# A transformer block in split float32 on one core: another order of work at the end of each MLP block, and of the loads behind the first MLP product

## The reference

```python
sh_a, sc_a, gt_a, sh_m, sc_m, gt_m = [m[:, None, :] for m in jnp.split(mod, N_MOD, axis=-1)]
...
h = rms_norm(x, g_pre_mlp[l]) * (1.0 + sc_m) + sh_m
y = jnp.square(jax.nn.relu(h @ w_mlp_in[l])) @ w_mlp_out[l]
x = x + gt_m * rms_norm(y, g_post_mlp[l])
```

## Time and profile before

| | us |
|---|---|
| median of 3 runs (2080.5 to 2085.15) | 2080.77 |
| the profiled execution | 2085.15 |
| its span, first to last instruction | 2083.5 |
| TensorE busy | 2025.0 (97%) |
| VectorE busy | 1717.7 (82%) |
| ScalarE busy | 992.3 (48%) |

### The profile page before, as it was taken

How to read it: one execution, slowest core, us unless ns; L and a number is a source line. 1 busy time by engine, 2 the same in 40 slices (tenths; PEclk the granted TensorE clock), 3 DMA queues, 4 the chain that set the end, 5 groups by cost and what they waited for, 6 DMA issues and landing times.

```text
span 2083.5 us, 30862 instructions
## 1 busy us (share of the span) xinstructions
PE 2025.0 (97%) x11186; PEld 1762.6 (85%) x11186; DVE 1717.7 (82%) x2013; ACT 992.3 (48%) x1403; POOL 156.4 (8%) x163
## 2 busy tenths in 40 slices
PE   7999999999999989999999999999999999999998
PEld 6887888877888868889999999998778888888886
DVE  5986898788876768689999999987788888888866
ACT  5554322578833365455555656654333333333322
POOL 0000000057600000000000000000020000000000
PEclk9999999999999999999999999999999999999999
DMA  9996869610286744757667666677656456446452
GB/s 308 341 310 221 272 204 256 200 31 1 72 293 213 264 149 139 241 179 235 216 218 231 214 231 214 216 241 287 256 211 242 179 184 242 181 181 249 174 182 81
DMA packets 294238, 435.37 MB, mean 209 GB/s; under 512 B 30181, under 2 KB 176265, under 8 KB 285321
## 3 DMA queue, kind: packets, MB, share of 16 engines
q1 hardware_dynamic: 276008, 361.43, 52.3%
q0 software_dynamic: 16704, 67.11, 8.8%
q10 hardware_dynamic: 1440, 5.70, 0.7%
HBM read 367.09 MB, written 67.11 MB: 208 GB/s over the span
## 4 chain that ended last, share of the span: by engine, by line
PE 77%; DVE 9%; DMA 5%; issue 4%; ACT 4%; SPq 1%; DVEq 0%; ACTq 0%
PE bank L2841 8%; PE bank L2843 8%; PE bank L2842 8%; PE bank L2863 7%; PE bank L2865 7%; PE bank L2864 7%; PE bank L2382 4%; PE bank L2384 4%; PE bank L2383 4%; PE bank L2395 2%; PE bank L2396 2%; PE bank L2397 2%; DMA raw<-in_w_ada 2%; DMA raw<-in_w_out 1%; PE bank L2921 1%
## 5 line engine op out<-in xcount | busy, mean ns | idle before, releaser
L2863 PE MATMUL bank<-hi,y_use 128*128 128x512 f32 x784 | 310.2, 396 | 13.6 <-DVE lo L2198 8.0
L1366 ACT ACTIVATE hi<-w 128x1024 fp32r<-128x1024 f32 x168 | 178.3, 1062 | 295.9 <-PE bank L2865 217.7
L2864 PE MATMUL bank<-lo,y_use 128*128 128x512 f32 x784 | 306.7, 391 | 0.0
L2865 PE MATMUL bank<-hi,y_use 128*128 128x512 f32 x784 | 306.6, 391 | 0.0
L1280 ACT ACTIVATE hi<-a 128x1024 fp32r<-128x1024 f32 x182 | 191.8, 1054 | 147.3 <-DVE a L2079 126.1
L2076 DVE TENSOR_TENSOR lo<-a,hi 128x1024 fp32r<-128x1024 f32 x182 | 221.9, 1219 | 43.9 <-ACT hi L1280 43.6
L837 ACT ACTIVATE hi<-raw 128x1024 fp32r<-128x1024 f32 (+2 forms) x132 | 129.1, 993 | 269.9 <-DMA raw<-in_w_in 93.7
L2198 DVE TENSOR_TENSOR lo<-w,hi 128x1024 fp32r<-128x1024 f32 x168 | 205.3, 1226 | 39.8 <-ACT hi L1366 38.2
L2841 PE MATMUL bank<-h_hi,hi 128*128 128x256 f32 x832 | 235.6, 283 | 0.0
L2842 PE MATMUL bank<-h_lo,hi 128*128 128x256 f32 x832 | 235.5, 283 | 0.0
L2843 PE MATMUL bank<-h_hi,lo 128*128 128x256 f32 x832 | 235.4, 283 | 0.0
(11 more groups left out here) (378 smaller groups left out, 4719.1 us busy)
## 6 DMA issues: line engine op xcount, KB each, us to landing
raw<-in_w_ada SPq DMA_DIRECT2D x166, 512.0 KB, 5.3
w<-in_w_mlp_out SPq DMA_DIRECT2D x128, 512.0 KB, 4.8
y_dram<-y_out POOLq DMA_DIRECT2D x32, 1792.0 KB, 6.8
y_use<-y_dram SPq DMA_DIRECT2D x53, 1024.0 KB, 8.8
a<-in_w_mlp_in SPq DMA_DIRECT2D x104, 512.0 KB, 4.5
raw<-in_w_in SPq DMA_DIRECT2D x32, 512.0 KB, 5.7
raw<-in_w_out SPq DMA_DIRECT2D x32, 512.0 KB, 5.0
gate_row<-in_w_ada SPq DMA_DIRECT2D x26, 512.0 KB, 5.1
```

The costliest lines, as they stand in the source:

```text
L2863: mm(bank[b + m][:], yh, hi[s][:, q, :], start=j == 0, stop=False)
L2864: mm(bank[b + m][:], yh, lo[s][:, q, :], start=False, stop=False)
L2865: ins = mm(bank[b + m][:], yl, hi[s][:, q, :], start=False, stop=j == PAIRS - 1)
```

## The change

It reorders four lists and neither adds nor removes an instruction. SyncE, at the boundary: the two halves of w21 and the last gate row are issued ahead of the first two y loads, the first half of w21 ahead of more weights. ScalarE, in each su block but the first: pair_hi goes ahead of snap 2 and su_hi 6. VectorE, at the end of each su block: su_low 0 of the next block ahead of its sum_one, and its sum_three behind corner 2 and su_low 2. VectorE, first half of the down phase: third(0) ahead of unit_lo(0), as in all other halves.

```diff
@@ -707,20 +707,20 @@
             end = SLOTS * (SU_BLOCKS - 1)
             sp.wait_ge(su_mixed, 4 * SU_BLOCKS - 1)
             weights(0, 0, "22", (0,))
+            sp.wait_ge(su_mixed, 4 * SU_BLOCKS)
+            weights(0, 0, "21", (0,))
             sp.wait_ge(su_lo, end + 5)
             weights(0, 0, "22", (1,))
             sp.wait_ge(w_used, SU_W + end + 2)
             weights(0, 0, "11")
             weights(0, 0, "12")
+            sp.wait_ge(su_lo, end + 6)
+            weights(0, 0, "21", (1,))
+            gate_behind(LAST, PAIRS - 1)
             sp.wait_ge(w_used, SU_W + end + 3)
             sp.wait_ge(y_saved, 16 * PAIRS)
             values(0, 0)
             values(0, 1)
-            sp.wait_ge(su_mixed, 4 * SU_BLOCKS)
-            weights(0, 0, "21", (0,))
-            sp.wait_ge(su_lo, end + 6)
-            weights(0, 0, "21", (1,))
-            gate_behind(LAST, PAIRS - 1)
             sp.wait_ge(w_used, DN_W)
             for k in (2, 3, 4):
                 values(0, k)
@@ -1324,10 +1324,10 @@
                 su_hi(g, i, 5)
                 if first:
                     square_pair(SU_FIRST - 1)
+                else:
+                    pair_hi(g, i - 1)
                 snap(g, i, 2)
                 su_hi(g, i, 6)
-                if not first:
-                    pair_hi(g, i - 1)
                 if final:
                     unit_hi(0, 0, 0)
                     unit_hi(0, 0, 1)
@@ -2139,14 +2139,14 @@
                 if final:
                     corner(g, i, 1)
                     return
+                su_low(g, i + 1, 0)
                 sum_one(g, i + 1)
-                su_low(g, i + 1, 0)
                 corner(g, i, 1)
                 su_low(g, i + 1, 1)
                 sum_two(g, i + 1)
-                sum_three(g, i + 1)
                 corner(g, i, 2)
                 su_low(g, i + 1, 2)
+                sum_three(g, i + 1)
                 if first:
                     pair_lo(g, i - 1)
 
@@ -2225,12 +2225,8 @@
                     wait_dn(dve, w_mixed, g, np, 8, 5 + h)
                     mix(dw["21"][np][h], dw["21"][np][h], dw["11"][np][h], ALU.subtract)
 
-                if first:
-                    unit_lo(0)
-                    third(0)
-                else:
-                    third(0)
-                    unit_lo(0)
+                third(0)
+                unit_lo(0)
                 third(1)
                 unit_lo(1)
                 one(0)
```

## The result

The kernel after takes 2101.85 us (median of 4 runs, 2100.46 to 2103.17), the kernel before, run beside it, 2080.64 (4 runs, 2080.5 to 2085.15). The ratio is 1.0098 (95% interval 1.0083 to 1.0113): 21.2 us slower. The forecast was 2089.6, with a range up to 2099. The direction held; the time lies outside the range.

A forecast was written before the change was run, and what follows sets the result against it. TensorE, busy 97%, was taken as the bound, time changing only through its waits. Loop + 16.4, second block + 0.4 and boundary - 8.0 gave + 8.8 us: 2089.6 against the median of 2080.77, range 2078 to 2099.

The forecast's parts named there:

- What bounds the kernel: Whole kernel: TensorE is busy 97% of the span, so time is lost or won only where it waits.
- The loop, + 16.4: su blocks: the path through VectorE and ScalarE closes at 20.95 us, 21 blocks wait, together 16.4 us slower.
- the walk: su block: measured start-to-start steps summed once around the longest path through VectorE and ScalarE, giving 20.95 us against 20.16.
- The second block, + 0.4: Where ScalarE's squares wait for pair_lo: between 1.2 us better and 0.8 worse, walked as 0.4 worse.
- SyncE at the boundary, - 8.0: After the su blocks: gate row lands earlier, 4.99 us gap goes, next gap shrinks, clock may stay up; 8.0 us gained.
- the delay of the values: Boundary: values 0, queued behind w21 half 1 and the gate row, land 2.6 or 3.3 us later, taken as 3.0.
- the earlier store: Boundary: pair_lo of the last pair, its store and the ten weight loads behind it move 4.6 us earlier.
- the boundary gives nothing back: Rival, boundary: values 0 land 5 us later, TensorE stops there, clock drops twice as before; 2097.6 us, chance 0.10.
- the four: Whole kernel: own forecast 2089.6 (0.72); rivals no closed path 2073.2 (0.12), boundary 2097.6 (0.10), lowered clock 2109 (0.06).
- third(0), nothing: First half of the down phase: unit_lo(0) moves to about 1427, covered because TensorE needs it only with values 0; no cost.
- The rival of a lowered clock in each block: su blocks: each short wait lowers the clock, 21 blocks lose 1.7 us each, + 36, total 2109 us; chance 0.06.

The follow-up runs named there:

- The two runs that split VectorE's edit: Kernel before with pair_hi moved up, plus either only sum_three behind su_low 2 (2084.21 us) or only su_low 0 ahead of sum_one (2115.72 us).
- the run with su_low 0 first: Kernel before with pair_hi moved up and su_low 0 ahead of sum_one, sum_three left in place: 2115.72 us, a single profiled execution.
- one number changed here: Kernel before with gate_part of the last block hung behind unit 7 in place of unit 2, no load moved: 2078.1 us, ratio 0.9977.

## Why the prediction was wrong in size

**What bounds the kernel: right.** What was lost or won beyond the scatter was TensorE's waiting, at the places named.

**The loop, + 16.4: right, 16.9.** Blocks of 20.91 to 20.99 (20.95 forecast), TensorE waiting for corner 1 (c_b), su_low 6 waiting 0.73 for ScalarE (0.75 forecast), pair_hi waiting for y_mix. The third block lost 1.03 where 0.65 was forecast; the second, which was to just meet its need, already waited 1.06 for corner 1. The path with ScalarE's edit alone came out as 20.55 to 20.63 (20.6), with VectorE's alone as 20.16 (closed). The two runs that split VectorE's edit moved the block in opposite directions, each to the length that the walk gave beforehand (20.16 and 21.48); neither a fixed cost for each edit nor VectorE's busy time, 18.45 to 18.61 us in a block of each of these kernels, does that. VectorE's 8% of idle time was no room for this order.

**The second block, + 0.4: wrong, + 2.3.** "ScalarE's squares wait there for pair_lo" was the only wait named. pair_hi, moved up, also waits for its output buffer: 3.47 us for the store of y, with snap 2 and su_hi 6 now behind it. ScalarE's edit alone has 1.8 of it, VectorE's alone 0.5. The bound given, 0.8 worse, was too narrow.

**SyncE at the boundary, - 8.0: this is the step that failed; it gave 2.2 at most, by the ratio of SyncE's edit alone 0.6.** Two terms of it were wrong, the delay of the values and the earlier store. On the first the sentence was "They land later by 1.05 MB at 410 GB/s, 2.6 us, or 3.3 us", and the loads landed 6.4 to 6.9 us later. The bytes were right and half 0 was rightly left out (0.54 us of waiting with it alone). The rate was wrong. In the run of SyncE's edit alone, from 1424.9 to 1434.4 (TensorE stood for the last 6.6 us of it), with the store of y under way, the queues carried (packets, MB, share of the DMA engines):

```profile
q1 hardware_dynamic: 420, 2.47, 62.1%
q0 software_dynamic: 387, 1.57, 40.1%
```

q1 moved 2.47 MB in 9.5 us, 260 GB/s, and not all of it for the loads up to the one waited for. The 1.05 MB cost about 6 us, 175 GB/s: w21 half 1 and the gate row landed 5.6 us behind the load ahead of them. The 410 of the earlier trace rows is both queues together, and the 317 of the earlier trace rows is a mean over 26 us of which the store takes only a part. Before the store's first packets q1 had the engines to itself, here in the kernel before, 1418.2 to 1424.2 us, 370 GB/s:

```profile
q1 hardware_dynamic: 947, 2.22, 102.8%
```

The store's first packets come 17.1 to 17.8 us behind the last block's start in all fourteen profiles, and the first y load landed at +20.4 before. So what was put ahead of it was paid for in the store's stretch. The Trainium skill (DMA: Bandwidth & Descriptors, Queues, rings and completion order) gave the direction, that descriptors of a ring are consumed in order, and the runs agree; the estimate of 2.9 us from its HBM limit did not hold (6.4 to 6.9 measured), since that limit is for all queues and one of them was asked for; all together they reached 410 to 428 GB/s in windows of this case. What the prediction left unused stands in the same section of that page: each DMA engine takes turns between the queues that have work, a packet at a time. The two rows agree (420 packets on q1, 387 of the store, which had 39% of the bytes), and read that way a load on q1 never has the whole rate while the store runs.

The second term was "pair_lo of the last pair, its store, SyncE's wait for that store ... and the ten weight loads behind it move 4.6 us earlier". Counted from the last block's start the store was issued at +41.0 where it was +41.1, and ScalarE shows why: the weight units ahead of pair_lo now wait for TensorE, which started 6.9 us late. The store before and after, and the first of these waits:

```profile
1449.36 0.94 POOL L3049 DMA_DIRECT2D y_dram<-y_out  x1 [27.28 <-DVE y_out L2033]
1466.88 0.94 POOL L3045 DMA_DIRECT2D y_dram<-y_out  x1 [27.15 <-DVE y_out L2033]
1457.62 1.06 ACT L1366 ACTIVATE hi<-w 128x1024 fp32r<-128x1024 f32 x1 [3.81 <-PE bank L2861]
```

So the next half began when it had begun before (+68.2, +68.5), the two gaps were only exchanged for one of 7.1 and two of 1.1, and what is left as a gain is a lower clock once instead of twice, which the second profile of the kernel before shows without any change. The rival "the boundary gives nothing back" had the mechanism, TensorE stopping at the values instead, with 5 us of delay (6.4 to 6.9 measured) and two drops of the clock (one was measured). It had been given a chance of 0.10. Its 2097.6 was the nearest of the four, 4.3 us under the measured median.

**third(0), nothing: right in effect.** It ran 18.8 us behind the last block's start, as forecast, and what waited behind it (unit_lo(0), corner 2) was done before the late values came. unit_lo(1) ended 3.6 us ahead of the first product.

**The clock.** Gaps of 0.57 us once in 21 us left it at 1.00, and so did those of up to 1.1 in the run with su_low 0 first. The rival of a lowered clock in each block is out.

**What is left.** With the two sizes corrected the sum is + 16.9 + 2.3 - 2.2 = + 17.0, which puts the kernel after at 2097.6 against the median of before, 4.2 short of its own. The profiled execution of before was 4.5 above the median of its four runs and that of after 1.3 below its own, which is the difference between 21.2 and 15.4; where in the kernel it lies the profiles don't show. It is scatter between executions as far as they tell, no step of the change was found for it, and its cause stays open.

## What to carry to other kernels

When two engines hand work back and forth, walk the path through both once around before an instruction moves, at the measured start-to-start distances and with its output buffer among the waits: an order can close a loop over the bound with one engine at 88% and the other at 57%, and one more move can open it again. A load that goes ahead of another in a queue is priced by what that queue alone delivered in that very stretch, between two landings. What is to move earlier must not hang on the engine that the same change makes late. And where an engine waits for data that nobody needs yet, move its waiting instruction back in its own list before transfers are moved forward: one number changed here gained 4.7 us, the loads put ahead of the values nothing that can be told, the gate row moved up behind them 3.1.

## What the runs showed that was not expected

The 0.52 MB loads at the boundary landed 3.0 and 2.6 us apart while the store of y was under way (run of SyncE's edit alone: w12 at +17.4, w21 half 1 at +20.4, the gate row at +23.0, the first y load, of 1.05 MB, at +26.8). The y load needed no more than 3.8 us for twice the bytes. The store too took longer with those loads ahead, landing at +30.3 where it was +27.5. The packets of the two queues while the y load was under way, 1430.5 to 1434.3 us, fit this:

```profile
q1 hardware_dynamic: 149, 1.09, 67.8%
q0 software_dynamic: 139, 0.55, 35.4%
```

The packets are about equal in number and those of q1 twice as large. In the stretch before, 1424.9 to 1430.5 us, with w21 half 1 and the gate row under way, they were 269 and 245, with 1.36 and 1.00 MB. So beside a store a load seems to be paid by its packets more than by its bytes. No run varied the packet size alone.

A gap that is taken away tends to come back at the next wait that was in its shadow: with the first gap cut from 4.99 to 1.57 and 1.61, the next half's grew from 2.99 to 4.71 and 4.94, and half of the gain was gone.
